# A hybrid decoder block with product-key experts in one core: 48 instead of 32 tokens of the last chunk in row dots, searches of two chunks interleaved, and 24 instead of 18 low parts made early

## What is computed

```python
def peer(xn, w_query, sub_keys, expert_u, expert_v):
    q = (xf @ w_query).reshape(t, 8, 2, 128)
    scores = jnp.einsum('thpk,hpnk->thpn', q, sub_keys)
    v1, i1 = lax.top_k(scores[:, :, 0], 16)
    v2, i2 = lax.top_k(scores[:, :, 1], 16)
    cand = (v1[..., :, None] + v2[..., None, :]).reshape(t, 8, 256)
    best, pos = lax.top_k(cand, 16)
    e1 = jnp.take_along_axis(i1, pos // 16, axis=-1)
    e2 = jnp.take_along_axis(i2, pos % 16, axis=-1)
    experts = (e1 * 128 + e2).reshape(t, 128)          # of 16384
    gates = jax.nn.softmax(best, axis=-1).reshape(t, 128)
    # for each token, over its 128 experts:
    a = gelu(einsum('cd,ced->ce', xc, expert_u[ic])) * gates
    return einsum('ce,ced->cd', a, expert_v[ic])

def reference(x, ...):
    h = x + hybrid_mixer(rmsnorm(x, norm_mix_g), w_in, conv_w, w_conv_out, pool_w, pool_scale, w_pool_out, w_out)
    h = h + peer(rmsnorm(h, norm_ffn_g), w_query, sub_keys, expert_u, expert_v)
    return rmsnorm(h, norm_final_g)
```

## Time and profile before

| | us |
|---|---|
| median of 3 runs (1600.41 to 1601.59) | 1601.42 |
| the profiled execution | 1600.42 |
| its span | 1598.6 |
| PE busy in the span | 1588.1 (99%) |
| DVE busy | 1291.2 (81%) |
| ACT busy | 701.3 (44%) |
| POOL busy | 410.8 (26%) |

### The profile page before, as it was taken

The page is one execution under the profiler, slowest core; times in us unless marked ns, Lnnn a source line. Parts: engine busy times, 40 slices in busy tenths (PEclk is TensorE's granted clock), DMA queues, the critical chain, the costliest instruction groups (busy, mean ns, idle before and its releaser), DMA issues.

```text
span 1598.6 us, 25446 instructions
## 1 busy us (share of the span) xinstructions
PE 1588.1 (99%) x8590; PEld 1403.5 (88%) x8590; DVE 1291.2 (81%) x2373; ACT 701.3 (44%) x936; POOL 410.8 (26%) x345
## 2 busy tenths in 40 slices
PE   9999999999999999999999999999999999999998
PEld 8888888888888999999999999998888888888886
DVE  6967833334578888988999998779999999999997
ACT  5444533333334433334677676433334333333334
POOL 1011100000000111103332322544454555455451
PEclk9999999999999999999999999999999999999999
DMA  5477632223322799967999999999999999999994
GB/s 215 146 245 241 232 105 101 96 92 106 109 85 71 243 321 349 333 211 272 330 410 397 392 389 383 409 357 368 387 405 400 409 413 403 398 411 397 400 368 158
DMA packets 150269, 461.82 MB, mean 289 GB/s; under 512 B 15888, under 2 KB 46656, under 8 KB 148544
## 3 DMA queue, kind: packets, MB, share of 16 engines
q1 hardware_dynamic: 82080, 231.08, 39.4%
q0 software_dynamic: 47920, 174.12, 28.8%
q10 hardware_dynamic: 20208, 55.94, 9.2%
HBM read 402.78 MB, written 58.29 MB: 288 GB/s over the span
## 4 chain that ended last, share of the span: by engine, by line
PE 97%; DMA 1%; ACT 1%; DVE 1%; issue 0%; SPq 0%; DVEq 0%; ACTq 0%
PE bank L1032 20%; PE bank L1033 20%; PE bank L1034 20%; PE bank L1220 11%; PE bank L1219 11%; PE bank L1218 11%; PE bank L1195 3%; PE bank L1098 1%; DMA w_lo<-early_dram 1%; DMA h_t<-x_t 1%; PE bank L1232 0%; ACT w_hi L685 0%; DVE w_lo L1271 0%; PE bank L1077 0%; PE bank L1079 0%
## 5 line engine op out<-in xcount | busy, mean ns | idle before, releaser
L685 ACT ACTIVATE w_hi<-w_raw 128x1024 fp32r<-128x1024 f32 x347 | 365.9, 1056 | 349.1 <-PE bank L1220 237.0
L1271 DVE TENSOR_TENSOR w_lo<-w_raw,w_hi 128x1024 fp32r<-128x1024 f32 x329 | 401.6, 1221 | 138.7 <-ACT w_hi L685 131.8
L1032 PE MATMUL bank<-xn_hi,w_hi 128*128 128x352 f32 (+1 forms) x1472 | 510.5, 347 | 2.7 <-DMA w_lo<-early_dram 2.7
L1033 PE MATMUL bank<-xn_lo,w_hi 128*128 128x352 f32 (+1 forms) x1472 | 504.7, 343 | 0.0
L1034 PE MATMUL bank<-xn_hi,w_lo 128*128 128x352 f32 (+1 forms) x1472 | 504.7, 343 | 0.0
L597 POOL DMA_INDIRECT rows<-u_rows,expert x128 | 156.1, 1220 | 646.8 <-DVE expert L1699 353.9
L1218 PE MATMUL bank<-w_hi,a_hi 128*128 128x512 f32 x768 | 298.8, 389 | 0.0
L1220 PE MATMUL bank<-w_hi,a_lo 128*128 128x512 f32 x768 | 298.8, 389 | 0.0
L1219 PE MATMUL bank<-w_lo,a_hi 128*128 128x512 f32 x768 | 298.8, 389 | 0.0
L1032 PEld LDWEIGHTS bank<-xn_hi,w_hi 128*128 128x128 f32 x1472 | 276.7, 188 | 20.7 <-issue 3.5
L1034 PEld LDWEIGHTS bank<-xn_hi,w_lo 128*128 128x128 f32 x1472 | 276.6, 188 | 17.6
(11 more groups left out here) (239 smaller groups left out, 1466.5 us busy)
## 6 DMA issues: line engine op xcount, KB each, us to landing
w_raw<-u SPq DMA_DIRECT2D x128, 512.0 KB
w_raw<-v SPq DMA_DIRECT2D x128, 512.0 KB
g_dram<-g_sb ACTq DMA_DIRECT2D x12, 2048.0 KB
g_in<-g_dram SPq DMA_DIRECT2D x84, 256.0 KB
act_dram<-act_out ACTq DMA_DIRECT2D x54, 352.0 KB
act_in<-act_dram SPq DMA_DIRECT2D x54, 352.0 KB
w_raw<-gate SPq DMA_DIRECT2D x32, 512.0 KB
w_raw<-w_in SPq DMA_DIRECT2D x31, 512.0 KB
```

The costliest lines, as they stand in the source:

```text
L685: act.activation(w_hi[:, slot, :], w_raw[:, slot, :], ACT.Copy).then_inc(hi_done, 1)
L1032: pe.matmul(out, hi, x_hi, start=k == 0, stop=False)
L1033: pe.matmul(out, hi, x_lo, start=False, stop=False)
L1271: dve.tensor_tensor(w_lo[:, slot, :], w_raw[:, slot, :], w_hi[:, slot, :].bitcast(F32), ALU.subtract).then_inc(lo_done, 1)
```

## The change

It raises `EXTRA` from 32 to 48, so `DU` falls from 352 to 336 columns, the rows of x of 48 tokens are spread, and the last three masks of 16 tokens have three parts instead of the last two. The stores to `x_rows_dram` are made in six pieces at six gathers. `EARLY_STEPS` goes from 9 to 12 and `EARLY_BUFFERS` from 3 to 4: four early low parts in each pass of the block loop. `search` takes two chunks and runs each phase for one and then for the other (`hold_at` waits for a mark, not for the newest instruction), with buffers for both. The tables of splits and dots are new: the search ends at U tile 45 instead of 52, 15 dots stand in it and 22 after it, and 51 are left for the V stage. The exponentials move from tile 54 to 47, the transposes of gates and expert numbers from tile 58 to 52.

```diff
-EXTRA = 32
+EXTRA = 48
-EXP_AT = 54
+TURN_AT = 13
-MASKS_X = EXTRA // MASKED
+MASKS_X = -(-EXTRA // MASKED)
+THREE_PARTS = MASKED * MASKS_X
-EARLY_STEPS = 9
+EARLY_STEPS = 12
+EARLY_LOOP = 10
-EARLY_BUFFERS = 3
+EARLY_BUFFERS = 4
-SEARCHES = (((3, 1, 1, 0), 0, 2), ((2, 1, 0, 1), 1, 2), ...
-BEFORE_FIRST = EXP_AT - 2
-DOTS_BEFORE = (1, 1, 1, 2, 1, 1, 1)
+QUERY_SPLITS = ((1, 1, 0, 1, 0, 0, 1), (1, 1, 0, 1, 0, 1, 0), (1, 1, 1, 1, 1, 0, 0), (2, 0, 1, 1, 1, 0, 0))
+LAST_SPLITS = ((2, 1, 1, 0, 1, 1, 0), (2, 0, 1, 1, 1, 0, 1), (2, 1, 1, 0, 2, 0, 0), (2, 1, 1, 0, 2, 0, 0))
+DOTS_FIRST = 1
+DOTS_SEARCH = (1, 2, 2, 2)
+DOTS_DECODE = (1, 2, 2, 2)
+BEFORE_FIRST = 45
+EXP_AT = BEFORE_FIRST + 2
+DOTS_BEFORE = (1, 2, 2, 1, 2, 2, 1, 2, 2, 1, 1, 1, 1, 2, 1)
-X_STORED, X_LOADED = 6, (12, 16)
+X_STORED = (4, 5, 6, 7, 8, 9)
+X_LOADED = (12, 13)
...
+    def mark(self):
+        return self.base + self.count
+    def hold_at(self, mark, carrier):
+        self.engine.wait_ge(self.sem, mark)
+        self.engine.sem_inc(carrier, 1)
...
-        early_hi = early("early_hi", [P, D], F32R)
+        early_hi = MemoryMap(nc, scratch_at)("early_hi", [P, D], F32R)
...
+            def store_x(g):
+                at = P - EXTRA + g * SHARED
+                pool.dma_start(x_rows_dram[g * SHARED:(g + 1) * SHARED, :, :],
+                               x_last[at:at + SHARED, :].unsqueeze(1).broadcast_to([SHARED, SPREAD, D])
+                               ).then_inc(x_rows_stored, 16)
...
                 early_split(i, 1)
                 split_weight(SLOTS * i + 6, 2, i + 2)
+                early_split(i, 2)
                 split_weight(SLOTS * i + 7, 3, i + 2)
                 u_high(i)
-                early_split(i, 2)
+                early_split(i, 3)
...
                 else:
                     early_rest(i, 1)
+                    early_rest(i, 2)
...
                 conv_low(i)
-                early_rest(i, 2)
+                early_rest(i, 3)
...
-                for k, u, half in rows_of:
-                    chain.did(dve.max(top_v[:, half, u, 0:8], row(k)))
-                chain.hold(held)
-                for k, u, half in rows_of:
-                    chain.did(dve.max_index(index(half, u)[:, 0:8], top_v[:, half, u, 0:8], row(k)))
-                    chain.did(dve.match_replace(less[:, k, :], top_v[:, half, u, 0:8], row(k), LOWEST))
-                splits[0]()
+                for s in both:
+                    for k, u, half in rows_of:
+                        chain.did(dve.max(top_v[:, s, half, u, 0:8], row(s, k)))
+                    done[s] = chain.mark()
+                for s in both:
+                    chain.hold_at(done[s], held)
+                    for k, u, half in rows_of:
+                        chain.did(dve.max_index(index(s, half, u)[:, 0:8], top_v[:, s, half, u, 0:8], row(s, k)))
+                        chain.did(dve.match_replace(less[:, s, k, :], top_v[:, s, half, u, 0:8], row(s, k), LOWEST))
+                    done[s] = chain.mark()
+                    splits[s]()
...
```

291 lines of the change are left out of this document (148 added, 143 removed).

## The result

| | before | with the change |
|---|---|---|
| median, us | 1600.97 (4 runs) | 1635.49 (4 runs, 1633.81 to 1639.73) |
| the profiled execution, us | 1600.42 | 1635.75 |
| its span, us | 1598.6 | 1633.6 |

The ratio is 1.0219, 95% interval 1.0200 to 1.0239: slower, by 34.5 us in the medians and by 35.0 in the spans of the two traces. The forecast was 1596.1 with a range of 1583 to 1608: the change went the other way, and the time lies outside the range.

The account below looks back on a forecast made before the run. TensorE's product spacings were taken to bound the kernel: -20.5 + 0.9 (third masks) + 15.8 - 2.7 + 1.2 = -5.3 from 1600.4 gives 1595.1, and 1.0 more for the median, 1596.1 us; range 1583 to 1608.

Parts of the forecast that it names:

- Columns: U stage: 16 fewer columns a product save 6.69 ns on each of 3072 products, 20.5 us off TensorE's path.
- weight loads set the spacing: Rival, U stage: 336 columns take as long as 352, giving 1616.6 us; chance 0.04.
- Queue of early parts: Projections: GpSimd's back-to-back stores and reloads, 6.44 us each, make the third pooling group late, +15.8 us.
- the queue keeps up: Rival, projections: with a cycle below 5.4 us only a 2.4 us hand-over delay stays, giving 1582.7 us; chance 0.17.
- Row stores in six pieces: U stage: 512 KB pieces between gathers instead of one 2 MB store end TensorE's read-back waits, -2.7 us; bounds 0 and -2.7.
- VectorE until the masks: 440 to 760 us: VectorE keeps room despite thirteen more dots ahead of the rounds, so TensorE isn't held, 0 us.
- the rounds: VectorE's 18.5 us of work fits TensorE's 18.7 for four tiles; +1.2 us charged from tile 45 on, bounds 0 and 8.
- budget of room: 440 to 760 us: VectorE's 24.5 us of waiting, less added and plus saved work, leaves 21 us, or 7 without search gains.
- memory or VectorE sets the pace from tile 45 on: Rival: the last 83 tiles don't get shorter, 13.3 us are lost, giving 1609.4 us; chance 0.16.
- the hand-over: Search: two chunks phase by phase remove most of the wait after each phase, 0.15 us each taken, +14 us of VectorE's room.
- V stage: Three more dots (3.5 us) and the rows in 86 tiles lie under VectorE's 17.8 us of waiting there: nothing.

Follow-up runs that it names:

- e1: The changed kernel, but GpSimd reloads an early buffer one store later, after issuing the next store: 1622.51 us, ratio 1.0126 to the kernel before.
- e6: The kernel before with one part of the change alone, 24 early low parts, four in a pass, four buffers: 1621.24 us, ratio 1.0128.
- e7: The kernel before with twelve chained copies on ScalarE ahead of the pooling groups' mix_hi, so TensorE idles once: 1617.11 us, ratio 1.0101.
- e3: The changed kernel, but the 48 x rows are stored once (196 KB) and repeated by eight small loads a group: 1626.94 us, ratio 1.0163.
- e5: The changed kernel, but the 3 MB of x rows are stored by eight DMAs, each two copies of all 48 rows: 1620.63 us, ratio 1.0126.
- e8: The changed kernel with both the later reload of e1 and the x rows cut by copies of e5: 1601.43 us, ratio 1.0007.

## Why the prediction was wrong

**Columns: right.** 6.67 ns off a product against 6.69, 20.5 us against 20.5. The rival that weight loads set the spacing is out: they were busy 49.61 of 50.00 us and 16 columns still came off in full. By that rule, the Trainium skill's (Perfetto Trace Analysis, Identifying the Most-Contended Engine), there was no room.

**Queue of early parts, +15.8: the step right, a term missing.** The cycle was 6.59 us for 6.44, the last reload at 203.2 for 200.1, the third pooling group at 211.3 for 208.4, and e1 and e6 show the cause. The waits are 15.1 us. What the sum lacked is the clock behind each stall, 5.4 us here in two places, 1.4 in e7. The rival by which the queue keeps up is out: it wanted a cycle below 5.4 us. The estimate by the Trainium skill (DMA: Bandwidth & Descriptors, Anatomy of one DMA) was 3.2 us for a landing, and the loads of this trace have a median of 4.9. (Rows 5 are loads and stores of the buffers together; the loads before had 4.7 us and not 4.4. It moves the sum by 0.3 us.)

**Row stores in six pieces, -2.7: wrong in its sign.** "The pieces are spread, so I take all of it" looked at how many bytes stand in the way at once and not at what such a store does to all that shares the DMA engines with it. The trace before could have warned. The 350 GB/s that this step names is about what the page's slices of 40 us have (321 and 349); while the 2 MB landed (13.0 us, 161 GB/s) all traffic together stood near 200 GB/s (582 to 596 us in 40 slices), and the earlier trace rows shows a read-back late behind it:

```profile
GB/s 184 106 31 0 257 246 187 187 211 199 199 211 199 211 211 199 234 187 199 199 199 211 199 199 222 199 222 316 339 410 421 351 281 222 234 363 445 410 400 411
```

The ends, 0 and -2.7, had excluded a loss without a reason. It was +16.9 against the pace (e3 and e5 take all of it back but 0.4), or +13.7 against the kernel before, 16.4 us away from the forecast.

**VectorE until the masks, 0, and the rounds, +1.2: mis-sized.** In tiles 44 to 64 the new kernel lost 14.4 us, behind them 5.2, together 19.6 against 1.2 with bounds 0 and 8. The step that failed is the budget of room: 21 us over 440 to 760 us, summed over the whole stretch, though 22 dots stand in its last 55 us, 0.4 a us, where 8 stood in the last 31, 0.26 a us. VectorE did lack the rows and not the time, which a budget of VectorE's time can't see:

```profile
DVE rows L1705 <- DMA rows<-u_rows,expert_extra: 5.3, 4, 2.1
DVE rows L1698 <- DMA rows<-u_rows,expert: 5.2, 4, 2.5
```

(waits of VectorE with the change, 715 to 790 us). The rounds themselves kept TensorE's pace, 18.7 us for four tiles; most of the 5.2 us arose in the plain tiles behind them, where VectorE waited for rows too. The trace before had that sign, in a line that the prediction didn't look at (waits of VectorE, 990 to 1065 us):

```profile
DVE rows L1662 <- DMA rows<-u_rows,expert: 14.5, 15, 2.6
```

So the rival "memory or VectorE sets the pace from tile 45 on", priced at 13.3 us, was right that something other than TensorE would set the pace behind tile 45, and wrong in its place: not late masks in the rounds, but late rows ahead of them and behind them. Its price took the rounds and plain tiles not to get shorter at all, which they did; that it is near the 17 us of e8 is luck. (In the same step the hand-over was read as 1.01 us for 0.8 of work; the row has 0.87, so 0.14 us a phase, close to the 0.15 that the sum took.)

**V stage: right** with 51 and up to 54 dots left, and closer to its edge than thought: 58 cost 13 us.

In sum, step by step, measured less forecast: projections 21.0 - 15.8 = 5.2; row stores 13.7 + 2.7 = 16.4; from tile 44 on 19.6 - 1.2 = 18.4, the largest; columns 0: 40.0 us, of 35.0 + 5.3 = 40.3 in the spans. The profiled execution took 1635.75 us where the sum said 1595.1, 40.7 more.

## What to carry to other kernels

Before work of the busiest engine is traded for gathers, ask what the rows need: their bytes at the rate of the stretch, and the number of row buffers over the landing time, and look whether the engine that uses them already waits for them. A DMA share of 1.0 answers neither: here the kernel had it before the change too. A queue that waits for the landing of what it has just issued runs at one landing after another; wait one piece later. Cut a store with repeats along the repeats, as e5 did, and not along its partitions. To every long stall of TensorE add 1.5 to 3 us for the clock.
